# Tail stage of a two-layer trunk: later turning of tiles on ScalarE, and layer 1's output weights loaded by the stage that uses them

## The reference, cut to what is computed

```python
for l in range(DEPTH):                                   # DEPTH = 2
    sh1, sc1, g1, sh2, sc2, g2 = modulation(cond, ada_w[l], ada_b[l])
    mix = mixer_l(h * (1.0 + sc1) + sh1)                 # ends in "@ w_out" (1024 x 1024)
    h = layer_norm(DN_ALPHA * h + g1 * mix, ln_g[l, 0], ln_b[l, 0])
    u = h * (1.0 + sc2) + sh2
    h = layer_norm(DN_ALPHA * h + g2 * ec_moe(u, moe_router[l], ...), ln_g[l, 1], ln_b[l, 1])

def ec_moe(h, router, w1, w3, w2):
    cap = 2 * N // 16
    aff = softmax(h @ router)                            # over the 16 experts, per token
    gate, idx = top_k(aff of each expert over its tokens, cap)
    ...                                                  # SwiGLU experts on the chosen rows
```

## Time and profile before

| what | us |
|---|---|
| median of three runs | 4874.97 (4870.78 to 4875.6) |
| the profiled execution, its own time | 4874.97 |
| its span, first to last instruction | 4873.2 |
| TensorE matmul busy in the span | 4323.1 (89%) |
| VectorE busy | 1320.7 (27%) |
| ScalarE busy | 769.0 (16%) |
| Tail of layer 0, TensorE's first and last matmul | 1182.18 to 1390.87 |
| VectorE takes the second half of tile 1, layer 0 | at 1213.77 |
| first top-k round behind the softmax of tile 7, layer 0 | at 1342.42 |
| the same two points in layer 1 | at 3463.93 and 3592.59 |

### The profile page before, as it was taken

The page is one execution under the profiler, slowest core; times in us unless marked ns, Lnnn a source line. Parts: engine busy times, 40 slices in busy tenths (PEclk is TensorE's granted clock), DMA queues, the critical chain, the costliest instruction groups (busy, mean ns, idle before and its releaser), DMA issues. The chain is left out here.

```text
span 4873.2 us, 60681 instructions
## 1 busy us (share of the span) xinstructions
PE 4323.1 (89%) x26349; PEld 3527.3 (72%) x26349; DVE 1320.7 (27%) x3042; ACT 769.0 (16%) x1987; POOL 154.6 (3%) x132
## 2 busy tenths in 40 slices
PE   8899979899949999999963999899949999999991
PEld 4667765584449999999962455454529999999991
DVE  5324442343630000000015243342470000000005
ACT  0112221100311111111111111111211111111110
POOL 0000000000000000000000000000000000000000
PEclk8999989999969999999986999999979999999995
DMA  6310001313137777777767000101316777777773
GB/s 271 122 56 29 16 13 31 119 59 114 52 130 270 265 268 273 267 268 271 263 225 300 23 22 24 41 22 47 144 61 232 269 261 273 269 270 265 268 269 100
DMA packets 150803, 796.79 MB, mean 164 GB/s; under 512 B 15496, under 2 KB 52008, under 8 KB 104522
## 3 DMA queue, kind: packets, MB, share of 16 engines
q1 hardware_dynamic: 139274, 755.16, 41.4%
q0 software_dynamic: 11264, 37.76, 3.6%
HBM read 733.52 MB, written 59.34 MB: 163 GB/s over the span
## 5 line engine op out<-in xcount | busy, mean ns | idle before, releaser
L1588 PE MATMUL PS<-arena 128*128 128x144 f32 x11264 | 1445.5, 287 | 10.2 <-ACT arena L524 10.2
L1588 PEld LDWEIGHTS PS<-arena 128*128 128x128 f32 x11264 | 1407.7, 191 | 11.8 <-ACT arena L524 10.4
L1573 PE MATMUL PS<-arena 128*128 128x144 f32 x5632 | 742.2, 286 | 0.0
L1573 PEld LDWEIGHTS PS<-arena 128*128 128x128 f32 x5632 | 711.5, 190 | 0.0
L1659 DVE TENSOR_TENSOR arena<-PS,arena 128x144 f32<-128x144 f32 x352 | 108.3, 308 | 2090.2 <-ACT arena L1631 2090.2
L1631 ACT ACTIVATE arena<-PS 128x144 f32<-128x144 f32 x352 | 104.9, 298 | 1606.8 <-PE PS L1588 1606.8
L1842 PE MATMUL PS<-arena 128*128 128x512 f32 x576 | 262.4, 611 | 28.1 <-DMA arena<-odd_w_in 28.1
L524 ACT ACTIVATE arena<-PS,arena 128x128 f32<-128x128 f32 x720 | 234.1, 452 | 294.0 <-PE PS L1551 200.9
L1856 PE MATMUL PS<-arena 128*128 128x512 f32 x576 | 257.0, 609 | 23.6 <-DMA arena<-odd_w_in 23.6
L1280 PE MATMUL PS<-arena 128*128 128x512 f32 x576 | 258.5, 603 | 5.4 <-POOLq L182 4.9
L1856 PEld LDWEIGHTS PS<-arena 128*128 128x128 f32 x576 | 112.4, 196 | 165.8 <-issue 141.3
(11 more groups left out here) (296 smaller groups left out, 3520.9 us busy)
## 6 DMA issues: line engine op xcount, KB each, us to landing
arena<-expert_panels SPq DMA_DIRECT2D x352, 1536.0 KB, 6.3
arena<-ada_w SPq DMA_DIRECT2D x12, 4096.0 KB, 16.1
arena<-odd_w_in SPq DMA_DIRECT2D x16, 1024.0 KB, 7.8
arena<-hgrn_w SPq DMA_DIRECT2D x20, 512.0 KB, 3.9
arena<-filter_spectra SPq DMA_DIRECT2D x36, 256.0 KB, 2.6
expert_sum<-arena SPq DMA_DIRECT2D x18, 512.0 KB, 7.9
mid_rows<-arena SPq DMA_DIRECT2D x18, 512.0 KB, 2.9
arena<-expert_sum SPq DMA_DIRECT2D x18, 512.0 KB, 5.3
```

The source lines that it names most:

```text
L1573: m = pe.matmul(PS[:, m_ // 3, m_ % 3 * SLOTS:m_ % 3 * SLOTS + SLOTS], s.w2[n % RING][:, m_ * P:(m_ + 1) * P], s.hid[:, f, :], start=f == ...
L1588: m = pe.matmul(PS[:, 6 + n % 2, q * 256:q * 256 + SLOTS], s.w13[n % RING][:, q, k, :], s.xs[e % 2][:, k, :], start=k == 0, stop=k == KD - 1)
```

## The change

In Tail.act the loop of ScalarE is written in another order, in both layers. Pass i now is: exp of tile i-2 (from i = 2), square root of tile i, first half of tile i, act_turn(i-1) (from i = 1). After the loop come exp of tile 7, act_turn(8) and exp of tile 8. The wait for the scales (s.cok) moves from ahead of the loop to behind the first half of tile 0. TensorE's and VectorE's orders stay.

In layer 1 the two transfers of w_out move from Retention.sync, where load_next and its wait are taken out, to Tail.sync, between the three transfers of x and those of the gates. TensorE's Tail then begins with a wait for both. In layer 0 nothing of this changes (s.l is 0). The source access pattern is written in another way for the same rows; the destinations are the same.

```diff
--- before.py
+++ after.py
@@ -1239,7 +1239,7 @@
                 s.zero = at(take(D), D)
                 assert o[0] <= FREE, o
                 sm = lambda n: sem(f"tl_{n}")
-                s.gl, s.cl = sm("rows_in"), sm("cols_in")
+                s.wl, s.gl, s.cl = sm("w_in"), sm("rows_in"), sm("cols_in")
                 s.xl = [sm(f"x_in{b}") for b in range(3)]
                 s.mf, s.ge = sm("proj_full"), sm("proj_evac")
                 s.var, s.sd, s.sc = sm("var"), sm("sd"), sm("norm_scale")
@@ -1250,9 +1250,16 @@
                 s.ch, s.pt = sm("chosen"), sm("picks_turned")
                 s.zok, s.zst, s.cok = sm("zero"), sm("zeroed"), sm("scales")
 
+            def load_w(s, sp, half):
+                w = I["even_w_out"] if s.l == 0 else I["odd_w_out"]
+                return sp.dma_start(s.W[half], w[0, 512 * half:512 * half + 512, :].rearrange("(k p) n -> p k n", p=P))
+
             def sync(s, sp):
                 for i in range(3):
                     sp.dma_start(s.x[i], rows_of(ORDER[i], s.l)).then_inc(s.xl[i], 16)
+                if s.l:
+                    for half in range(2):
+                        s.load_w(sp, half).then_inc(s.wl, 16)
                 for c in range(2):
                     sp.dma_start(s.g[:, c, :], modD[s.l, c:c + 1, 2 * D:3 * D].to_broadcast((P, D))).then_inc(s.gl, 16)
                 sp.dma_start(s.w, I["moe_router"][s.l].rearrange("(k p) e -> p k e", p=P)).then_inc(s.cl, 16)
@@ -1312,6 +1319,8 @@
                 pe.transpose(PS[0:E_N, 7, i % 4 * P:i % 4 * P + P], s.aff[:, ORDER[i], :], ident).then_inc(s.af, 1)
 
             def pe(s, pe):
+                if s.l:
+                    pe.wait_ge(s.wl, 32)
                 s.project(pe, 0, 0)
                 s.project(pe, 0, 1)
                 for i in range(1, NT):
@@ -1348,17 +1357,21 @@
                 act.activation(a, a, ACT.Exp).then_inc(s.ex, 1)
 
             def act(s, act, ch):
-                act.wait_ge(s.cok, 1)
                 for i in range(NT):
                     st = s.st[i % 2]
+                    if i >= 2:
+                        s.act_exp(act, i - 2)
                     act.wait_ge(s.var, i + 1)
                     act.activation(st[:, 15:16], st[:, 14:15], ACT.Sqrt).then_inc(s.sd, 1)
                     act.wait_ge(s.sc, i + 1)
                     act.activation(s.h[:, ORDER[i], 0:512], s.x[i % 3][:, 0:512], ACT.Identity,
                                    bias=st[:, 17:18], scale=st[:, 16:17]).then_inc(s.na, 1)
                     if i:
-                        s.act_exp(act, i - 1)
-                    s.act_turn(act, i)
+                        s.act_turn(act, i - 1)
+                    elif i == 0:
+                        act.wait_ge(s.cok, 1)
+                s.act_exp(act, NT - 2)
+                s.act_turn(act, NT - 1)
                 s.act_exp(act, NT - 1)
 
             def dve_half(s, dve, ch, i, n):
@@ -1735,8 +1748,8 @@
 
 
         class Retention:
-            def __init__(s, uT, yT, base, wts):
-                s.uT, s.yT, s.wts = uT, yT, wts
+            def __init__(s, uT, yT, base):
+                s.uT, s.yT = uT, yT
                 o = [base]
 
                 def take(n):
@@ -1778,7 +1791,7 @@
                 s.uf, s.ub = sm("upd_full"), sm("state_ok")
                 s.of, s.oe, s.var, s.sd, s.yo = sm("o_full"), sm("o_read"), sm("o_var"), sm("o_sd"), sm("y_ok")
                 s.yf, s.yv = sm("y_t_full"), sm("y_t_evac")
-                s.st, s.wo = sm("state_stored"), sm("next_w_in")
+                s.st = sm("state_stored")
 
             def sync(s, sp):
                 for dst, src in ((s.rope, I["rope"]), (s.dist, I["time_dist"]), (s.prow, I["pos_rows"]),
@@ -1805,17 +1818,9 @@
                         src = s.Sf[1] if d == 1 else s.Sf[0]
                         for a in range(2):
                             sp.dma_start(O["new_state_ret"][0, 0, d, h, a * P:(a + 1) * P, :], src[:, a, :]).then_inc(s.st, 16)
-                        if h == C_H - 1 and d == 1:
-                            s.load_next(sp)
-                sp.wait_ge(s.wo, 32)
                 sp.wait_ge(s.st, 64 * C_H)
 
-            def load_next(s, sp):
-
-                sp.wait_ge(s.wu, 2 * C_H)
-                w = I["odd_w_out"][0].rearrange("(h k p) n -> h p k n", h=2, p=P)
-                for half in range(2):
-                    sp.dma_start(at(s.wts[half], 4, D), w[half]).then_inc(s.wo, 16)
+
 
             UPD, OUT = (4, 0, 1, 2), (5, 7)
 
@@ -2088,7 +2093,7 @@
                 at(o + 144 + 2 * n, n, parts=CAP_C).bitcast(U32), at(o + 144 + 3 * n, n, parts=CAP_C))
         aff0, pick0 = picks(9216)
         aff1, pick1 = picks(27648)
-        wts0, wts1 = (29184, 16384), (0, 4096)
+        wts0 = (29184, 16384)
         conv0 = HyenaFold(hv, hx1, yT0, wts0)
         blocks = [[
             Front(Modulation(0, [at(8192 + b * 8192, KD, D) for b in range(2)], FREE - 2048)), MixerInput(0, uT0, 9216),
@@ -2103,8 +2108,8 @@
         next_block()
         experts1 = Experts(1, h1, pick1, 28032, 0)
         blocks.append([
-            MixerInput(1, uT1, 9216), Retention(uT1, yT1, 18432, wts1),
-            Tail(1, yT1, h1, wts1, 40320, 42368, aff1, pick1, experts1), experts1, MoeEnd(1, h1, 28032, None),
+            MixerInput(1, uT1, 9216), Retention(uT1, yT1, 18432),
+            Tail(1, yT1, h1, (0, 4096), 40320, 42368, aff1, pick1, experts1), experts1, MoeEnd(1, h1, 28032, None),
         ])
         nums = sorted(v.num for v in pool)
         assert nums == list(range(nums[0], nums[-1] + 1))
```

## The result

The changed kernel takes 5047.95 us (median; 5047.47 to 5049.5) against 4873.19 us (4870.78 to 4875.6) for the one before: a ratio of 1.0359, with a 95% interval of 1.0341 to 1.0377. It is slower by 174.8 us. The forecast was 5057 us, the range 5024 to 5078 us.

The account below looks back on a forecast made before the run. TensorE, 89% busy, was taken as the bound, with VectorE later from Tail's tile 6. Loops 166.8, weights 16.5, clock 0.6 and Retention -1.8 sum to 182.1 us on 4874.97: 5057 us, range 5024 to 5078.

Parts of the forecast that it names:

- the half clock through logits: In both Tails, the clock stands at 0.50 through logits after each wait; logits take 3.56 us instead of 1.85.
- the lost wait for the table: In Tail's softmax, VectorE no longer waits for ScalarE's Exp table, whose load takes 1.28 us.
- the gain in Retention: With w_out's issues gone from Retention, VectorE waits less for the store beside them: -1.8 us (between 0 and -1.8).
- the signs that the prediction named as wrong: In Tail: a wait under 7 us, a clock returning within logits, or a landing time other than 16.5 us.
- The wait per tile: In Tail, TensorE idles ahead of logits until the late act_turn ends: 7.48 us from the end of project(i, 1).
- The loss by the clock: In Tail, each restart behind a wait costs 4.07 us: 1.71 in logits, 2.36 in dense passes; 28.5 us a layer.
- Rival (1): In Tail, logits count for the clock's return, so a restart costs 2.36 us in all: 5033 us, chance 0.22.
- The loops: Tail's tile loops grow by 83.4 us a layer, waits and clock together: +166.8 us for two (bounds 135 and 177).
- The weights: At layer 1's Tail start, TensorE waits for w_out: +16.5 us, and +0.6 us for the clock behind it.
- The cover that the prediction named: In layer 1's Tail, the norm's columns come some 10 us later, but tile 0's first half comes later still; 4 us spare.
- (2): In Tail, the clock doesn't fall, or its fall is hidden: 4996 us, chance 0.04.
- (4): In Tail, TensorE gets past waiting logits to project(i+1, 0): 4867 us, some 4884 with w_out exposed; chance 0.03.

Follow-up runs that it names:

- the filled wait: The changed kernel with ten extra unused matmuls on TensorE ahead of logits(0) to logits(7), filling the idle time: 5001.15 us.
- the early passes alone: The changed kernel, but from tile 6 on ScalarE turns a tile in its old place, so only passes 1 to 5 stay late: 4998.76 us.
- the run with the weights alone: The kernel before with only layer 1's w_out load moved to Tail, ScalarE's order as before: 4890.7 us.
- the run with the order alone: The kernel before with only ScalarE's new order in Tail, layer 1's weights still loaded in Retention: 5030.26 us.
- TensorE's new order: The changed kernel with project(i+1, 0), the next tile's first half, put ahead of logits(i-1) on TensorE: 4935.01 us.
- the kernel with twelve: The changed kernel with twelve extra unused matmuls, in place of ten, ahead of logits(0) to logits(7): 4999.81 us.

## Why the prediction was right, and where its terms were off

**The mechanism** held in each step that it named: the wait of logits for L524 in passes 1 to 8, the half clock through logits, the lost wait for the table, the wait for the weights. Only the gain in Retention, a side term, wasn't there. Each part alone, the filled wait and the early passes alone measured it, and each came within some 8 us of its own forecast; those of the parts alone were taken from the changed kernel's own trace, so that they test only whether the parts add. By two of the signs that the prediction named as wrong, its sizes were off: the idle rows of passes 1 to 5 are under its 7 us in 8 of 10 cases (6.93 and 6.98 us), and the weights landed later than its 15.9 to 17.1 us.

**The wait per tile** was 7.48 us in the prediction and is 7.09 to 7.14. Two things were put too high: L524's first instruction starts 0.09 us before L1367 ends (1244.75 against 1244.03 + 0.81), and the handoff to TensorE takes 0.05 to 0.1 us, not 0.33; the last 0.02 us are L524's 2.88 us in place of 2.90. Over 16 waits this is 6 us.

**The loss by the clock** was 4.07 us for a restart and is 3.75: 1.70 us in logits, as predicted (3.40 against 1.70 us from their start to the next projection's), and 1.41 to 2.80 us in the projection behind, 2.05 on the mean of 14 (8.52 to 9.91 us against 7.11), where 2.36 was taken from restarts elsewhere. Over 14 restarts this is 4.5 us. Rival (1), in which logits count for the clock's return and a restart costs 2.36 us in all, is refuted by its size, and 5033 us by the result. The rule behind it, the slow phase as a budget of time (the Trainium skill, "TensorE: Matmul & The Clock Gate", section "Part 1: The HAM clock gate"), did not hold for narrow matmuls: through the 3.40 us of logits the clock stood at 0.50, and the dense passes behind them had a loss of their own nearly as large as that of a whole restart.

**The loops** together: predicted 166.8 us, measured 156.9.

**The weights**: predicted 16.5 + 0.6 us, measured 17.5 us to tile 1's second half. The sum is right by luck, as two errors cancel. TensorE's start came 17.57 us behind SyncE's first issue, 1.1 us over the 16.5 and outside the range given for it. The 0.6 us for the clock were not lost: 48 passes took 22.53 us, and 22.56 before. The cover that the prediction named held: VectorE waited 19.3 us for the columns, and then still 5.5 us for TensorE's first half of tile 0.

**The gain in Retention** is the term that failed. I gave w_out's transfer the blame for a wait of 4.06 us behind a store in the last head, and took off 1.8 us. Without the transfer the wait is still 3.78 us in the same place, in VectorE's timeline:

```profile
3483.11 0.87 DVE L2062 SCALAR_TENSOR_TENSOR arena<-arena,PS 128x256 f32<-128x256 f32 x2 [3.78 <-DMA new_state_ret_out<-arena]
```

So 0.3 us came back at most, and the other runs show that not even that is the transfer's: without it in Retention this wait is 4.31 us in the run with the weights alone, and with it 3.48 us in the run with the order alone.

```profile
3402.39 0.87 DVE L2058 SCALAR_TENSOR_TENSOR arena<-arena,PS 128x256 f32<-128x256 f32 x2 [4.31 <-DMA new_state_ret_out<-arena]
...
3483.13 0.87 DVE L2061 SCALAR_TENSOR_TENSOR arena<-arena,PS 128x256 f32<-128x256 f32 x2 [3.48 <-DMA new_state_ret_out<-arena]
```

What makes this store slower than those of other heads was not tried and stays open.

In sum: 182.1 - 9.9 (loops) + 0.4 (weights) + 1.5 (Retention) = 174.1 us, against 173.0 in the span; the last us is the start of layer 0's Tail, which lies 0.8 us earlier in this execution.

**The rivals**: (2), no loss by the clock, would have been 4996 us, and filling the wait showed what it is worth. (4), no wait, fell with the first row of logits. No matmul overtook. The run with TensorE's new order comes nearest to what overtaking would have given, and at 4935 us it is far from the 4884 us of this rival with w_out exposed, as passes 6 to 8 still lose.

## What to carry to other kernels

On an engine that runs its queue in order, look at what stands behind an instruction before its input is made later, even if the engine that makes it has time to spare: here ScalarE was 16% busy, its work didn't change, and a step of 2.9 us moved behind another cost 11 us a tile in passes 1 to 5 and 8 in the others. Price such a wait with the restart of the clock: here 3.75 of the 11 us. If the input has to be late, move ready work ahead of the waiting instruction (112.9 us here), and where an engine waits for a table or a handoff, put its own independent work into the gap (9.5 us here).

## What the runs showed of the hardware that was not expected

The clock fell not only in long gaps. Logits are 16 passes of 16 columns that take 1.85 us at full clock. With 1.60 to 1.67 us of idle time ahead of them it fell in 3 of 4 places (the kernel with ten extra matmuls); with 0.48 to 0.55 us in 1 of 10 (the same kernel); with 0.30 to 0.38 us in 2 of 4 (the kernel with twelve); and with TensorE's new order it fell in one of the early passes of each layer, where 0.54 and 0.62 us of idle time stood between logits and turning on one side and the projection on the other. With no idle time ahead of logits or right behind them it never fell, neither in the 10 early passes with twelve extra matmuls nor in the kernel before (1.00 in the earlier trace rows). The Trainium skill, "TensorE: Matmul & The Clock Gate", section "Why this matters for your kernels", advises against long idle gaps between bursts of matmuls; here narrow matmuls beside a gap of 0.30 to 0.62 us were enough in some passes, and not in others with the same gap. What makes the difference, and whether it is the narrowness of logits, was not tried by itself.
